# Hybrid mLSTM and attention layer: output tiles transposed by DMA, edge masks on VectorE, output weights scaled on GpSimd

## What is computed

```python
y_m = mlstm_merge(hm, om, mlstm_norm)            # RMS over each head's 128 columns, * sigmoid(o)
# attention: keys within |i-j| <= 128, all 256 context keys, one sink logit
p = softmax(concat([s_band, s_ctx, s_sink]))
y_a = p @ concat([v_band, v_ctx])
x = x + g_a * (concat([y_m, y_a], axis=-1) @ w_out)
x = x + g_f * conv_glu(modulate(rmsnorm(x, norm_ffn), sh_f, sc_f), w_up, ffn_conv_w, ffn_conv_b, w_down)
```

## Time and profile before

| | |
|---|---|
| median of three runs | 1046.06 us (1045.25 to 1046.52) |
| profiled execution, its own time | 1048.59 us |
| its span, slowest core (core 0) | 1046.8 us |
| all cores | 1031.8 to 1046.8 us |
| TensorE busy | 858.4 us, 82% |
| VectorE busy | 645.6 us, 62% |
| ScalarE busy | 456.8 us, 44% |
| GpSimd busy | 334.5 us, 32% |

### The profile page before, as it was taken

One profiled execution on the slowest core, in us unless ns is written; L12 is line 12 of the kernel. 1 busy time (PEld: TensorE's weight loads), 2 busy tenths in 40 slices (PEclk: granted clock), 3 DMA queues, 4 the chain that ended last, 5 costly groups with the idle time before them and its releaser, 6 DMA issues.

```text
span 1046.8 us, 18654 instructions; the slowest of 8 cores (1031.8 to 1046.8 us)
## 1 busy us (share of the span) xinstructions
PE 858.4 (82%) x5868; PEld 470.9 (45%) x5868; DVE 645.6 (62%) x1259; ACT 456.8 (44%) x764; POOL 334.5 (32%) x395
## 2 busy tenths in 40 slices
PE   0448975897978862787776999999999999999994
PEld 0325543453444432444443555445554555455551
DVE  0135643676666778878783665556665565667785
ACT  2257633666556532655685443114420243124442
POOL 2123543016456574555552421003210122011111
PEclk9968998899989995888798999999999999999997
DMA  9963199690000024111126542014310233011122
GB/s 160 218 170 101 42 102 138 90 117 1 2 2 1 2 35 88 50 52 61 42 81 111 92 64 48 2 25 77 61 21 1 41 61 61 1 31 61 61 103 99
DMA packets 35741, 67.41 MB, mean 64 GB/s; under 512 B 3136, under 2 KB 19520, under 8 KB 35136
## 3 DMA queue, kind: packets, MB, share of 16 engines
q0 software_dynamic: 27008, 37.79, 24.3%
q1 hardware_dynamic: 8640, 28.43, 8.2%
HBM read 95.60 MB, written 8.39 MB: 99 GB/s over the span
## 4 chain that ended last, share of the span: by engine, by line
PE 61%; DVE 11%; DMA 11%; issue 8%; ACT 4%; POOL 4%; DVEq 0%; POOLq 0%; ACTq 0%; SPq 0%
PE pp L687 40%; PE pp L1613 15%; DMA wada<-w_ada 3%; DMA adst<-w_ada 3%; DMA xbuf<-x 2%; DVE acc L863 1%; DVE yt L1373 1%; ACT pT L1155 1%; PE pp L1150 1%; DVE Cst L1075 1%; PE pp L1179 1%; DMA wout<-w_out 1%; DVE Cst L1081 1%; DVE hsum L1358 1%; DVE acc L867 1%
## 5 line engine op out<-in xcount | busy, mean ns | idle before, releaser
L687 PE MATMUL pp<-hxT,wub 128*128 128x410 bf16 (+3 forms) x1760 | 310.2, 338 | 3.1 <-DMA wub<-w_up 3.1
L687 PEld LDWEIGHTS pp<-hxT,wub 128*128 128x128 bf16 x1760 | 171.9, 98 | 140.1 <-issue 5.5
L1613 PE MATMUL pp<-wdb,gT 128*128 128x512 bf16 x704 | 157.4, 384 | 6.1 <-DVE gT L1576 6.0
L1551 ACT ACTIVATE fac<-pp,ffcw 128x410 f32<-128x410 f32 (+1 forms) x110 | 76.2, 692 | 175.8 <-PE pp L687 175.8
L1618 DVE TENSOR_TENSOR x<-pp,x 128x512 f32<-128x512 f32 x128 | 88.6, 692 | 86.8 <-PE pp L1613 86.7
L1573 ACT ACTIVATE fth<-fac 128x410 f32<-128x410 f32 (+1 forms) x110 | 59.5, 541 | 120.9 <-DVE fac L1566 120.9
L1613 PEld LDWEIGHTS pp<-wdb,gT 128*128 128x128 bf16 x704 | 69.4, 99 | 90.5 <-issue 10.7
L1576 DVE TENSOR_TENSOR gT<-fth,pp 128x410 bf16<-128x410 f32 (+1 forms) x110 | 62.8, 577 | 60.6 <-PE pp L687 53.0
L1155 ACT ACTIVATE pT<-pp 128x1024 bf16<-128x1024 f32 x78 | 75.4, 1030 | 53.2 <-PE pp L1150 52.0
L209 POOL DMA_DIRECT2D wub<-w_up x22 | 12.4, 563 | 219.1 <-PE pp L687 215.9
L1160 POOL TENSOR_TENSOR pT<-pT,mneg 128x1024 bf16<-128x1024 bf16 x30 | 67.3, 2251 | 42.4 <-ACT pT L1155 42.3
(11 more groups left out here) (168 smaller groups left out, 1314.3 us busy)
## 6 DMA issues: line engine op xcount, KB each, us to landing
wub<-w_up POOLq DMA_DIRECT2D x22, 512.0 KB, 5.2
xbuf<-x SPq DMA_DIRECT2D x16, 512.0 KB, 5.5
adst<-w_ada POOLq DMA_DIRECT2D x16, 512.0 KB, 11.1
xb<-x SPq DMA_DIRECT2D x16, 512.0 KB, 3.5
out<-x SPq DMA_DIRECT2D x16, 512.0 KB, 2.7
wdb<-w_down POOLq DMA_DIRECT2D x22, 256.0 KB, 5.1
wada<-w_ada POOLq DMA_DIRECT2D x8, 512.0 KB, 21.8
wq<-w_qk POOLq DMA_DIRECT2D x8, 256.0 KB, 16.0
```

The lines of the kernel that those rows point to most:

```text
L687: ins = e.matmul(ps1(b)[:, c0:c0 + n], lhs(k), rhs(k), start=(k == 0), stop=(k == KC - 1))
L1551: kb.op("act", lambda e: e.activation(ac[:, 0:m], ps1(ba)[:, o0 - i0:o1 - i0], AF.Identity, bias=ffcw[:, c, 3:4], scale=ffcw[:, c, 1:2]), ...
L1613: ins = e.matmul(ps1(b), bufof[gk[i]][:, T * 128:(T + 1) * 128], bufof[ws[i]][:, half * 512:(half + 1) * 512], start=(i == 0), stop=(c == ...
```

## The change

Five edits. A new helper `dmat` issues a DMA transpose from the SyncE queue. (1) `attn_fin` transposes `yat` into `ya[T]` by DMA instead of TensorE and VectorE. (2) `mlstm_tile` transposes `yt` into `ymT` by DMA instead of TensorE and ScalarE, and `yt` has two buffers. (3) The 30 edge masks are multiplied on VectorE; tile, mask and result are bf16. (4) `scale_wout` runs on GpSimd. (5) `proj_v` may run 12 tiles ahead, with rank 0.0; `ktm` has three buffers, for which the last `pT` buffer is given up.

```diff
+    def dmat(self, out, in_, reads=(), writes=(), dur=2.4):
+        q = "sp"
...
+            return e.dma_start_transpose(out=out, in_=in_)
...
+        self.efree[q] = t0 + 0.6
+        self.dma_free[q] = s + 0.8
+        self.etime[tok] = s + dur
...
+    KTM1_AT = pT_at.pop()
...
-    ktm = [... for i in range(1)]
+    ktm = [... for i, a in enumerate((HXC_AT, KTM1_AT, KTM1_AT + 1024))]
...
-        yield Req("pe", hk_ + ["wv"], banks=1, when=lambda: ti <= prog["fin"] + 8, rank=0.1)
+        yield Req("pe", hk_ + ["wv"], banks=1, when=lambda: ti <= prog["fin"] + 12, rank=0.0)
...
         if mi is not None:
-            yield Req("pool", [pk])
-            kb.op("pool", lambda e: e.tensor_tensor(
+            yield Req("dve", [pk])
+            kb.op("dve", lambda e: e.tensor_tensor(
...
-                reads=[pk, ("mneg", mi)], writes=[pk], dur=2.2)
+                reads=[pk, ("mneg", mi)], writes=[pk], dur=0.75)
...
-        yield Req("pe", [yk], banks=1)
-        bt_ = kb.take()
-        transposes(yt, [yk], 4, bt_)
+        yield Req("sp", [yk])
+        kb.dmat(ya[T][:], yt[:], reads=[yk], writes=["ya%d" % T])
         R_yat.give(yk)
-        yield Req("dve", [PS(bt_)])
-        kb.op("dve", lambda e: e.tensor_copy(ya[T][:], psb(bt_)[:, 0:512]...
...
-            yield Req("dve", ["wout%d" % k, ("gabc", 0), ("gabc", 1)], slack=2.0)
-            kb.op("dve", lambda e, k=k: e.tensor_tensor(wout[k][:], wout[k][:], gabc[:], ALU.mult),
+            yield Req("pool", ["wout%d" % k, ("gabc", 0), ("gabc", 1)], slack=2.0)
+            kb.op("pool", lambda e, k=k: e.tensor_tensor(wout[k][:], wout[k][:], gabc[:], ALU.mult),
...
-    R_yt = Ring(["yt0"])
+    R_yt = Ring(["yt0", "yt1"])
...
-        yield Req("pe", [(yk, h) for h in range(4)], banks=1, rings=[R_ym])
-        b = kb.take()
+        yield Req("sp", [(yk, h) for h in range(4)], rings=[R_ym])
         mk = R_ym.take()
-        transposes(bufof[yk], [(yk, h) for h in range(4)], 4, b)
+        kb.dmat(bufof[mk][:], bufof[yk][:], reads=[(yk, h) for h in range(4)], writes=[mk])
         R_yt.give(yk)
-        yield Req("act", [PS(b)])
-        kb.op("act", lambda e, b=b, mk=mk: e.copy(bufof[mk][:], psb(b)[:, 0:512]...
```

More of the change, by code:

```diff
@@ L220, in dma, with fn @@
             self.end_tokens.append(tok)
+        return tok
+    def dmat(self, out, in_, reads=(), writes=(), dur=2.4):
+        reads = list(reads)
+        writes = list(writes)
+        q = "sp"
+        i = self.dma_slot_next[q]
+        self.dma_slot_next[q] = (i + 1) % self.nslots[q]
+        key = ("dma", q, i)
+        waits, est = self._deps(q, reads, writes)
+        pv = self.dma_slot_val[key]
+        if pv > 0 and self.waited[q].get(key, 0) < pv:
+            self.waited[q][key] = pv
+            waits.append((key, pv))
+        self.dma_slot_val[key] = pv + 16
+        tok = (key, pv + 16)
+        def fn(e, out=out, in_=in_):
+            return e.dma_start_transpose(out=out, in_=in_)
+        self.ops[q].append((waits, fn, (key, 16)))
+        self._commit(tok, reads, writes)
+        t0 = max(self.efree[q], est + 0.06)
+        self.efree[q] = t0 + 0.6
+        s = max(self.efree[q], self.dma_free[q])
+        self.dma_free[q] = s + 0.8
+        self.etime[tok] = s + dur
         return tok
@@ L987, in build @@
         pT_at.append(pT_at[-1] + 2048)
+    KTM1_AT = pT_at.pop()
     pT = [kb.sb("pT%d" % i, [128, 2, 512], BF16, a) for i, a in enumerate(pT_at)]
-    ktm = [kb.sb("ktm%d" % i, [128, 4, 128], BF16, HXC_AT + 1024 * i) for i in range(1)]
+    ktm = [kb.sb("ktm%d" % i, [128, 4, 128], BF16, a) for i, a in enumerate((HXC_AT, KTM1_AT, KTM1_AT + 1024))]
     vwb = [kb.sb("vwb%d" % i, [128, 4, 129], BF16, HXC_AT + 1024 + 1056 * i) for i in range(2)]
@@ L1222, in scale_wout @@
         for k in ks:
-            yield Req("dve", ["wout%d" % k, ("gabc", 0), ("gabc", 1)], slack=2.0)
-            kb.op("dve", lambda e, k=k: e.tensor_tensor(wout[k][:], wout[k][:], gabc[:], ALU.mult),
-                  reads=["wout%d" % k, ("gabc", 0), ("gabc", 1)], writes=["wout%d" % k], dur=t_dve(1024))
+            yield Req("pool", ["wout%d" % k, ("gabc", 0), ("gabc", 1)], slack=2.0)
+            kb.op("pool", lambda e, k=k: e.tensor_tensor(wout[k][:], wout[k][:], gabc[:], ALU.mult),
+                  reads=["wout%d" % k, ("gabc", 0), ("gabc", 1)], writes=["wout%d" % k], dur=2.2)
             kb.made.add("wout%d" % k)
@@ L1239, in build @@
     r += 2048
-    yt = [kb.sb("yt0", [128, 512], BF16, r)]
-    r += 1024
+    yt = [kb.sb("yt%d" % i, [128, 512], BF16, r + 1024 * i) for i in range(2)]
+    r += 2048
     assert r <= ARENA, (r, ARENA)
@@ L1377, in mlstm_tile @@
         fs_free.append(fi)
-        yield Req("pe", [(yk, h) for h in range(4)], banks=1, rings=[R_ym])
-        b = kb.take()
+        yield Req("sp", [(yk, h) for h in range(4)], rings=[R_ym])
         mk = R_ym.take()
-        transposes(bufof[yk], [(yk, h) for h in range(4)], 4, b)
+        kb.dmat(bufof[mk][:], bufof[yk][:], reads=[(yk, h) for h in range(4)], writes=[mk])
         R_yt.give(yk)
-        yield Req("act", [PS(b)])
-        kb.op("act", lambda e, b=b, mk=mk: e.copy(bufof[mk][:], psb(b)[:, 0:512].rearrange("p (g t) -> p g t", g=4)),
-              reads=[PS(b)], writes=[mk], dur=0.62)
-        kb.give(b)
         ym_of[T] = mk
```

3 lines of the change are left out of this document (removed).

## The result

The change makes the kernel slower. It takes 1061.12 us (median of four runs, 1057.58 to 1064.67) where the kernel before took 1046.29 beside it: a ratio of 1.0139, 95% interval 1.0095 to 1.0182. The forecast was 1011 us with a range of 997 to 1035. Times are medians of all runs of a kernel, while ratios and intervals leave out runs in which the cores of one die ran at a lower clock, so a ratio can differ a little from the quotient of two times. The profiled execution took 1064.67 us, and its slowest core is core 7. First come its span and clock, then the same core by stage, in the windows that answer to the earlier trace rows; attention and seam are one window here.

The account below looks back on a forecast made before the run. It took TensorE's waits in attention, seam and mLSTM as the room to gain, the last stage being TensorE-busy; 17 + 9 + 9 = 35 us off the profiled 1048.59 gave 1013.6, or 1011 us by the median, range 997 to 1035.

Parts of the forecast that it names:

- Masks and stretching: Attention stage: masks cost VectorE 0.69 us each, 20.7 us in all; of 19.3 us of stretching, 16 us go.
- Attention, gain 17: Attention stage: shrinks from 152.3 to 135.2 us, a gain of 17 us, between 6 and 24.
- I strike the 13.4 us for `ktm`: Attention stage: with three `ktm` buffers, TensorE's 13.4 us of waiting for `ktm` disappears.
- Ahead of the tail TensorE has 114.4 - 13.3 = 101.1 us of work: Attention before its last 19 score blocks: 101.1 us of TensorE work plus 14.5 us of idle time, 115.6 us.
- Seam, gain 9: Between attention and mLSTM: earlier weight loads and GpSimd scaling leave about 3.5 of 12.3 us, gain 9, between 0 and 11.
- one landing of about 9, and 8 x 2.25 = 18 us of scaling: Attention's end: GpSimd's 31 us of issuing, landing and scaling runs mostly under some 26 us of remaining score blocks.
- Case E: Seam not freed, as VectorE's masks slow GpSimd's scalings: gains sum to 16 us, 1030 us; chance 0.05.
- mLSTM stage, gain 9: mLSTM stage: 6 us from scalings leaving VectorE plus 3 us balance from DMA transposes, between 20 and a loss.
- The term of 1.3 us per tile: mLSTM stage: DMA landing of 2.7 us replaces about 1.4 us, making each of 16 tiles' chains 1.3 us longer.
- TensorE's queue 19.7 us lighter ... I count 3 us for the balance: mLSTM stage: TensorE loses 6.8 us of transposes and 12.9 us of waiting; net of longer tile chains, 3 us gained.
- gain 6: mLSTM stage: four scalings, 5.9 us, leave VectorE's queue on the path to the first output projection, gaining 6 us.
- Case D: mLSTM stage: transpose landings delay 16 output projections, slower from 4.9 us on; 1056 us at 5.5 us; chance 0.08.

Follow-up runs that it names:

- the old order: Kernel before with only its mLSTM outputs transposed by DMA, every engine keeping the instruction order of before, one `yt` buffer: 1065.12 us, 1.0128 of before.
- the planner's new one: Kernel before with only its mLSTM outputs transposed by DMA, engines' order planned anew, two `yt` buffers: 1068.28 us, 1.0173 of before.
- the fastest kernel: Kernel before plus masks on VectorE, `ya` by DMA and three `ktm` buffers; value rank 0.1, mLSTM outputs and scaling as before: 1026.55 us, 0.9758 of before.

## Why the prediction was wrong

**Masks and stretching: right.** 0.682 us per mask (0.69 assumed), 0.697 us median for L1110, and the masks alone are worth 11 us of attention stage.

**Attention, gain 17: in size there, but not in this kernel.** In first to last `pT` it means 145.5 - 17 = 128.5 us; without the rank and the row of scalings it is 125.7. Two steps failed. The first is "I strike the 13.4 us for `ktm`" on account of three buffers and the values ahead: the masks alone do that. The second is "Ahead of the tail TensorE has 114.4 - 13.3 = 101.1 us of work". The tail was right to the block, 19 exponentials. But the step took TensorE as the bound ahead of it and kept only 14.5 us of waiting there. Putting values first makes ScalarE idle 18 us longer in exchange. The forecast never set the lead against no lead; it costs 12.0 us of stage.

**Seam, gain 9: the place right, the sign of the whole wrong.** The seam did fall, from 17.3 to 5.9 us. But "one landing of about 9, and 8 x 2.25 = 18 us of scaling" was costed as hidden, on an idle engine, beside a tail bounded by ScalarE. It blocks VectorE for 17 us and lengthens attention by 15.1 (137.9 with the scaling alone taken back, 153.0 in the change). The rows had shown the mechanism, and the forecast used it for the masks that went, not for the scalings that came. Case E asked whether VectorE would slow GpSimd; it is the other way round.

**mLSTM stage, gain 9: wrong by 25.** The term of 1.3 us per tile was right (in the old order 1.2 at the first tile, 1.0 as a mean of all 16, 2.5 at most), and the median landing was shorter than assumed. The step that failed is "TensorE's queue 19.7 us lighter ... I count 3 us for the balance". Of the 12.9 us of the earlier trace rows the row puts 10.1 down to `yt`, and moving the transposes away does not end that wait: TensorE's next instruction is the output projection, which needs the same `yt`, 1.2 us later. In the old order the transport costs 11.3 us, in the planner's new one, with a second `yt` buffer, 19. The "gain 6" from four scalings off VectorE's path came to nothing: 163.4 us with them and 163.3 without.

**The cases.** Case D named the right place, each transpose ahead of its projection with TensorE's queue behind. Its rule, a loss only from a landing of 4.9 us on, rested on the gains of the other parts and on the slack of three lanes, and both failed. The last stage was right: 480.5 and 481.1 us.

One after the other, from before to after, the ratio goes: masks -1.65%, `ya` by DMA -0.45%, `ktm` -0.3% (neither step is clear of the intervals, but with the values ahead `ya` by DMA is: 0.9878 against 0.9945), rank +1.2%, scaling on GpSimd +0.9%, mLSTM outputs by DMA +1.7%. That these add up to +1.4% is so by how they were made; that the last three are costs of their own shows the other way round, each taken out of the whole change alone: rank 1.1% (to 1.0027), scaling 1.0% (to 1.0038), outputs 1.7% (to 0.9969).

## What to carry to other kernels

When a wait at the head of a queue is for the data and not for the unit, moving the operation elsewhere does not end it: ask what the waiting engine would do next, and whether that needs the same data. Before work goes to an idle engine, look at which engine it was seen to hold up, and in how long a row it will run. And give work in a common queue a head start only if the engine it displaces was not the one that others wait for.

## What the runs showed of the hardware

A VectorE instruction can be held for far longer than one GpSimd instruction. Before, a 0.70 us scaling was held for the rest of one mask (2.12 us) and came through between two. Beside GpSimd's scalings with no pause it was held for the whole row: 16.5 to 17.0 us on each of eight cores, through the DMA issues in between too; and in the fastest kernel a cast of 0.43 us was held 5.0 us by four weightings. It was seen with two SBUF operands in f32 (`og`), with bf16 ones (mask), and with a single f32 operand (cast). By the records the held instruction can start 0.6 us ahead of the row. In all sixteen cases (eight of the changed kernel, eight of the fastest) GpSimd was issuing a DMA when it started, while the scaling that came through before had started inside a mask; whether that makes the difference was not tested. The Trainium skill, "SBUF — State Buffer", § Who interferes with whom, says that the two engines share a pair of ports under an exclusive lock, which an instruction keeps to its end while the other engine blocks. The traces agree on the blocking. They differ on its length, since a waiting instruction did not get in when the GpSimd instruction ended. Why it got in before and not here stays open.

The DMA transpose of 128x512 bf16 within SBUF landed 2.4 us after its issue in the median, and 10.5 at worst over the eight cores of the changed kernel (one of `yat`, on core 3); one issue occupies SyncE for 1.18 us, a plain one for 0.33. The Trainium skill, "VectorE: DVE Perf Modes", § The three transpose paths, gives 1309 ns for a 128x128 block, from which the forecast estimated 5.2 us for four in a row; the 2.4 us measured are less than half of that.
